# Products of constants on TensorE around the norms of a two-block transformer kernel

## The reference, cut to what matters

```python
# first block, per layer
h  = rms_norm(x, mix_norm_g[l]);  proj = h @ w_in[l]      # norm 0
...
x  = x + merged @ w_out[l]
h2 = rms_norm(x, mlp_norm_g[l])                            # norm 1
x  = x + square(relu(h2 @ w_up[l])) @ w_down[l]
# second block, per layer (a = 4 ** 0.25)
x = layer_norm(a * x + 0.5 * swiglu(x, ...), ...)          # norm 0
x = layer_norm(a * x + token_mixing(x, ...), ...)          # norm 1
x = layer_norm(a * x + cross_attention(x, mem, ...), ...)  # norm 2
x = layer_norm(a * x + 0.5 * swiglu(x, ...), ...)          # norm 3
```

## Time and profile before

| | |
|---|---|
| median of 3 runs | 2579.63 us (2578.45 to 2580.16) |
| profiled execution, first to last instruction | 2578.9 us |
| TensorE matmuls busy | 2391.2 us (93%), 16356 instructions |
| TensorE weight loads busy | 2194.2 us (85%), 16386 instructions |
| VectorE busy | 1418.0 us (55%) |
| ScalarE busy | 1146.1 us (44%) |
| GpSimd busy | 270.7 us (10%) |
| mean granted TensorE clock | 0.962 |

### The profile page before, as it was taken

One profiled execution on the slowest core, in us unless ns is written; L12 is line 12 of the kernel. 1 busy time (PEld: TensorE's weight loads), 2 busy tenths in 40 slices (PEclk: granted clock), 3 DMA queues, 4 the chain that ended last, 5 costly groups with the idle time before them and its releaser, 6 DMA issues.

```text
span 2578.9 us, 42911 instructions
## 1 busy us (share of the span) xinstructions
PE 2391.2 (93%) x16356; PEld 2194.2 (85%) x16386; DVE 1418.0 (55%) x1842; ACT 1146.1 (44%) x1792; POOL 270.7 (10%) x228
## 2 busy tenths in 40 slices
PE   6988998998999999899998889979999999987997
PEld 6978986887987998699997789879878999876996
DVE  4556555546654444555476564454465555765445
ACT  4744543663543443345343444434434434343443
POOL 0001200000110110100001221021110000221111
PEclk9999998999999999899998899989999999998998
DMA  6423554432553655334423335545544434252552
GB/s 201 146 83 117 186 193 146 164 115 82 178 185 140 216 183 191 136 137 174 163 100 131 131 128 183 199 154 187 198 143 166 159 108 169 81 175 95 181 197 98
DMA packets 56850, 394.46 MB, mean 153 GB/s; under 512 B 6678, under 2 KB 7040, under 8 KB 10944
## 3 DMA queue, kind: packets, MB, share of 16 engines
q1 hardware_dynamic: 52864, 377.98, 42.1%
q0 software_dynamic: 3776, 13.64, 1.7%
HBM read 391.24 MB, written 1.05 MB: 152 GB/s over the span
## 4 chain that ended last, share of the span: by engine, by line
PE 57%; DVE 4%; issue 4%; ACT 2%; DMA 0%; POOL 0%; DVEq 0%; SPq 0%; ACTq 0%; POOLq 0%
PE psum L372 51%; PE psum L691 2%; PE psum L721 2%; PE psum L1565 1%; PE psum L705 1%; DVE w_low L330 1%; ACT w_high L327 1%; PE psum L576 1%; DVE xT_low L629 0%; PE psum L398 0%; DVE gates L610 0%; DVE xs L1852 0%; DVE mx L747 0%; ACT attn_p L803 0%; DMA ring<-in_weights 0%
## 5 line engine op out<-in xcount | busy, mean ns | idle before, releaser
L330 DVE TENSOR_TENSOR w_low<-ring,w_high 128x1024 fp32r<-128x1024 f32 x704 | 882.3, 1279 | 647.8 <-ACT w_high L327 647.3
L372 PE MATMUL psum<-xT_high,w_high 128*128 128x256 f32 x3168 | 911.2, 288 | 35.4 <-DVE xT_low L629 20.9
L327 ACT ACTIVATE w_high<-ring 128x1024 fp32r<-128x1024 f32 x704 | 718.3, 1052 | 426.6 <-PE psum L372 390.3
L372 PE MATMUL psum<-xT_low,w_high 128*128 128x256 f32 x3168 | 905.0, 286 | 0.0
L372 PE MATMUL psum<-xT_high,w_low 128*128 128x256 f32 x3168 | 904.4, 285 | 0.0
L372 PEld LDWEIGHTS psum<-xT_high,w_high 128*128 128x128 f32 x3168 | 617.1, 195 | 39.0 <-DVE xT_low L629 19.6
L372 PEld LDWEIGHTS psum<-xT_low,w_high 128*128 128x128 f32 x3168 | 617.3, 195 | 0.2
L372 PEld LDWEIGHTS psum<-xT_high,w_low 128*128 128x128 f32 x3168 | 616.8, 195 | 0.0
L372 PE MATMUL psum<-w_high,hidden 128*128 128x512 f32 x1216 | 377.8, 390 | 9.7 <-DVE attn_pT L1841 5.2
L372 PEld LDWEIGHTS psum<-w_high,hidden 128*128 128x128 f32 x1216 | 228.2, 188 | 60.4 <-issue 11.8
L372 PE MATMUL psum<-w_low,hidden 128*128 128x512 f32 x608 | 236.6, 389 | 0.0
(11 more groups left out here) (212 smaller groups left out, 2284.9 us busy)
## 6 DMA issues: line engine op xcount, KB each, us to landing
ring<-in_weights SPq DMA_DIRECT2D x354, 1024.0 KB, 4.9
pages<-in_affine POOLq DMA_DIRECT2D x16, 512.0 KB, 5.9
ring<-in_weights SPq DMA_DIRECT2D x4, 880.0 KB, 4.4
pages<-in_mem POOLq DMA_DIRECT2D x2, 1024.0 KB, 5.2
x<-in_x_in SPq DMA_DIRECT2D x1, 1024.0 KB, 4.8
pages<-in_rows POOLq DMA_DIRECT2D x2, 512.0 KB, 7.3
y<-x SPq DMA_DIRECT2D x1, 1024.0 KB, 4.1
masks<-in_masks POOLq DMA_DIRECT2D x1, 640.0 KB, 8.3
```

What stands on the lines that cost most here:

```text
L327: eng.activation(high, raw, ACT.Copy).then_inc(*self.flag("w_rounded").one())
L330: eng.tensor_tensor(self.w_low[:, q % SPLITS, 0:w], raw, high.bitcast(F32), ALU.subtract).then_inc(*self.flag("w_split").one())
L372: m = pe.matmul(out, a, b, start=(first and i == 0), stop=(last and i == len(pairs) - 1))
```

## The change

A helper issues n matmuls of the constants. `norm_transposes` takes three counts: that many before the transposes of t = 0, before those of t = 1, and before the first products of the bank that comes next. Those around the transposes go to the columns of PSUM bank 7 from 256 + 128 t on, so they are 256 wide for t = 0 and 128 wide for t = 1; those after go to columns 0 to 255 of the bank that the next product group is about to write, behind the wait for that bank. All these columns are written again, with the accumulation started anew, before anything reads them. There is no new wait.

```diff
+        self.idle_after = 0
...
     def gemm_tokens(...):
         for t in range(NT):
             self.take_bank(pe, l, banks, (key, t))
+            self.next_bank_idle(pe, self.bank(banks, (key, t))[:, 0:SEQ])
...
     def gemm_features(...):
         out = self.bank(banks, group)
+        self.next_bank_idle(pe, out[:, 0:SEQ])
...
+    def idle_products(self, pe, out, n):
+        for _ in range(n):
+            pe.matmul(out, self.identb[:, :], self.masks[:, 0, 0:out.shape[1]], start=True, stop=True,
+                      skip_group_check=True)
-    def norm_transposes(self, pe, l, j, src):
+    def norm_transposes(self, pe, l, j, src, idle=(0, 0, 0)):
         for t in range(NT):
+            self.idle_products(pe, self.psum[:, 7, SEQ + t * P:2 * SEQ], idle[t])
             pe.wait_ge(*self.flag("xn_ready").at(l, NT * j + t + 1))
...
+        self.idle_after = idle[2]
+    def next_bank_idle(self, pe, out):
+        self.idle_products(pe, out, self.idle_after)
+        self.idle_after = 0
...
 # block 1
-            c.norm_transposes(pe, l, 0, c.xs)
+            c.norm_transposes(pe, l, 0, c.xs, (16, 30, 20))
-            c.norm_transposes(pe, l, 1, c.xs)
+            c.norm_transposes(pe, l, 1, c.xs, (4, 40, 16))
...
 # block 2
+            c.idle_after = 30
             ffn("f1", c.input_split(pe, l, None), 0)
-            c.norm_transposes(pe, l, 0, c.xs)
+            c.norm_transposes(pe, l, 0, c.xs, (4, 40, 28))
-            c.norm_transposes(pe, l, 2, c.xs)
+            c.norm_transposes(pe, l, 2, c.xs, (4, 40, 24))
-            c.norm_transposes(pe, l, 3, c.xs)
+            c.norm_transposes(pe, l, 3, c.xs, (4, 40, 0))
```

## The result

| | kernel before | changed kernel |
|---|---|---|
| median | 2578.45 us (7 runs, 2577.64 to 2580.16) | 2585.60 us (7 runs, 2583.88 to 2594.76) |
| profiled execution, first to last instruction | 2578.9 us | 2582.3 us |
| mean granted TensorE clock | 0.962 | 0.969 |

The ratio is 1.0032, with a 95% interval of 1.0022 to 1.0043: slower, 7.15 us in the medians, where 8.7 us of gain were forecast. The profiled execution of the changed kernel took 2583.88 us, the lowest of its seven. In all that follows, three executions that lay over 100 us above their neighbours are left out (3506.95 us of the changed kernel run again, 3276.78 and 2717.88 us of two others).

What follows compares the result with a forecast made beforehand. TensorE was taken to bound the kernel, its clock falling after waits at norms. Terms 2.8 + 1.1 + 1.7 + 0.4 + 2.7 + 0.8 - 0.8 gave 8.7 us gained, so 2570.9 us; range 2566 to 2576.

Steps and rivals of the forecast that it cites:

- Price of the constants: On TensorE at full clock, one product of constants takes 0.065 us for 128 columns and 0.12 us for 256; doubled when low.
- Rival 1: Products of 128 constant columns take 0.08 to 0.11 us, cutting the gain to 7.0 or 3.9; chance of 0.09 or more: 0.12.
- Start of the program: First products, of 512 columns, from 23.71 us: 14 run at full instead of low clock, gaining 2.8 us; lateness costs nothing.
- Norm 1 of block 1: Products after this norm run at full clock, less 0.4 us lateness: gains of 1.1 us in layer one, 1.7 in layer two.
- Norm 0 of layer two: In block 1: first product 1.6 us late, then full clock; net gain 0.4 us, between -0.5 and 2.0.
- Start of block 2: The first 28 products run at full clock, gaining 2.7 us; the 30 constants are covered by the wait for `w_low`.
- Norm 2: In block 2, twice: only the low stretch after the first products counts; 0.4 us gained each time, 0.8 in all.
- the fear that the text named: At norm 2 of block 2, TensorE idles 2 us twice, so the clock may fall again despite the 24 constants before.
- Norm 0 of block 2: Twice: faster products only lengthen the wait for `w_low` and the clock may fall; -0.8 us, between +0.5 and -1.6 for both.
- three signs of being wrong: Low stretches remaining at 238 and 646; t = 1 late by 1 us or more; `w_low` waits growing by what the norms gave.
- Rival 2: Weights or activations arrive no sooner and the clock falls elsewhere in block 2; half the sum goes, 2575.2 us; chance 0.17.
- Rivals 3 and 4: Constants fail to hold the clock up, near 28 us lost, 2607, chance 0.05; falls at norms have another cause, 2581, chance 0.04.

Runs made afterwards that it cites:

- after_again: The changed kernel run once more without any edit: nine executions, ratio 1.0029; the profiled execution took 2596.29 us.
- after_oc: The changed kernel plus nine 256-wide products of constants in the wait before `oc` in each layer of block 2: 2572.80 us, ratio 0.9976.
- the shifts: The kernel before with 4, 8 or 12 constants of 256 columns amid the `up` products of block 1: ratios 1.0029, 1.001 and 0.9989.

## Why the prediction was wrong, by its steps

**Price of the constants: right in kind, too high.** 0.056 us for 128 columns and 0.109 for 256 at the high clock, against 0.065 and 0.12. The first is below the lower bound of 0.06 that I had taken from half a product of 256 columns; the second was read off products of weights, which are slower (0.12). Rival 1 is out. The Trainium skill, "TensorE: Matmul & The Clock Gate", section "Back-to-back issue gap", states about 81 ns for sustained pairs; the forty pairs of this trace do not agree, with 56.

**Start of the program: right.** 2.8 us forecast; 2.75 by VectorE's fourth `w_low`, at 33.44 before and 30.69 after, and by TensorE's products from 34 us on.

**Norm 1 of block 1: clock right, size too high.** The prediction put the first four constants between the two sets of transposes; they lie ahead of both. From the first of them (226.94) to the transposes of t = 1 it is 3.56 us against 3.52, so the lateness was 0.04 and not 0.4. But products of weights at full rate ran into what feeds them: waits of 0.24 us for `xT_low` at 235.21 and 0.16 for `w_low` at 237.14. The lead grew by 0.5 us in layer one (forecast 1.1) and by 1.1 in layer two (1.7).

**Norm 0 of layer two: wrong low in this trace, nearer in others.** The forecast had t = 1 2.1 us late and the first product 1.6; from the first transposes to the first product it is 7.03 us against 6.87 before, 0.16 later. The lead grew by 2.1 us, about the upper bound that the text named (2.0), and not by 0.4, since the 30 constants took 2.3 us and not the 3.4 of the forecast, and the 20 behind them ran beside the evacuation. It depends on when the clock comes back, for which the prediction took 2.8 us of constants without a row that shows it: in the trace of after_again the same 30 take 3.20 us (423.73 to 426.93) and the first product comes 1.4 us late. Of the nine traces with block 1's constants, six have it 1.1 to 1.5 us late and gain 0.6 to 1.1 us here, and three have it in place.

**Start of block 2: right** in its place, 2.65 against 2.7 (a lead of 8.06 us becomes 10.7).

**Norm 2: nothing, where 0.8 was forecast.** The idle times are 1.79 and 1.81 us with the 24 constants done in between, and the low stretch is there again at 1494.20: the fear that the text named came true in full.

**Norm 0 of block 2: right sign, too small.** The wait for `w_low` in layer one grew from 2.18 us to 3.48, as the text had it, and the lead stayed 10.7 us. In layer two the wait grew from 1.36 to 2.62, and with the falls behind it 4.1 us went, where the bound for both layers was -1.6. This was no accident of one trace: all seven with these constants lose 4.1 to 4.3 us there.

These terms make 2.75 + 0.5 + 1.1 + 2.1 + 2.65 = 9.1 us. The other 1.6 us of the lead at 848 us came from low stretches in the attentions of block 1 that went away or moved: one at 87.87 us of before brought 1.57 us. The prediction counted none of these.

Summed up, the trace has 10.7 us won, 4.1 lost behind norm 0 and 9.5 at the compressors, and 0.5 in small steps: 3.4 us slower in the span, where 8.7 faster were forecast.

**The step that failed** is the sentence behind the sum: "Behind each of these places TensorE is dense and is what VectorE and ScalarE wait for, so a gain stays." A gain of time stayed for 1050 us. What did not stay was the clock in stretches that the change does not touch. The sum took each of them as fixed, as the one profile showed it. They are not fixed: of 89 executions of the kernel before, 23 lie 10 us higher (none of 7, then 13 of 31, 4 of 18, 4 of 23, 2 of 10). The three executions that I had were all of the lower kind, in which both layers pass the wait before `oc` at full clock; the trace showed these compressors at 1.00, and nothing in it showed how near they are to falling. The changed kernel has at least one layer hit in each of its 16 executions, by their times; two profiles confirm it, with one and two.

Where nine constants hold this place (after_oc) the change comes to 2572.80 us, inside the range of 2566 to 2576. The second step that failed is the term of norm 0 in block 2, -0.8 for both layers, which measured -4.1 in layer two alone.

None of the three signs of being wrong that the text named has come: the low stretches at 238 and 646 are gone, t = 1 is 0.04 us late, and the waits for `w_low` fell from 21.3 to 14.7 us. They all watched the places of the change, and the loss lay elsewhere.

**Rival 2** ("Clock kept, gain lost behind it ... the clock falls in the attentions and norms of block 2 at other places than before") was right in its second half, with the wrong price; the waits for `w_low` did not take the gain. I let it take half of the sum and so kept it above no change. A fall costs what follows it: 9.5 us here, more than the sum. Rivals 3 and 4 are out: the constants do hold the clock up, and the text's loss of 28 us does not appear.

**What stays open.** Why the phase of the changed kernel hits a compressor every time: the shifts show that 0.9 us can do it, not why. Why norm 0 of block 2 costs 4.1 to 4.3 us in layer two of every trace and 1.1 to 1.8 us between medians: the stretch that gives 2.9 us back in two traces is seen, not what makes it go. Whether the 16 products of 64 columns (1.89 us) that stand ahead of the wait before `oc` have a part in the falls: no run changed them. Whether the one-row bias products (L400, 1.74 us at 1896.81) lead to the falls at 1900.28, 1917.34 and 1944.42, which begin while TensorE is busy: no run left them out.

## What to carry to other kernels

When a stretch of narrow products follows a short wait, fill that wait first: nine products of constants in 1 us were worth 9.5 us in a hit layer, more than the 6.2 us that the norms together bring when that place is held. Count such fillers as the length of the wait over their measured spacing (0.109 us for 256 columns), and only where what follows is bound by TensorE. Before summing gains of the clock, run the kernel before some 20 times and shift it by a microsecond: if its times fall into groups, one profile shows one of them, and a small gain can change which.

## What was unexpected of the hardware

- Full TensorE activity did not mean full clock. The 64x15 products of a compressor ran at busy 1.00 and a granted clock of 0.50 for 13.15 us, and the whole low stretch, with transposes ahead and 5.3 us of wide products behind, lasted 20.5 us; the low stretches of the earlier trace rows, of wide products alone, last 3.23 to 6.04 us. The same 128 products ran at 1.00 for 6.89 us where they were entered at it.
- The same 1.02 us wait for the same tile is followed by a fall of the clock in 9 of 20 cases. The Trainium skill, "TensorE: Matmul & The Clock Gate", section "What's actually happening", says that the ramp depends on the run and costs under 1% of a typical kernel. The groups here, 10 us or 0.4% apart, agree with both, though they come from falls in the middle of the kernel; they are larger than the change.
- Pairs of a weight load and a bfloat16 product of 128 columns sustain 0.056 us, half of the 0.109 us for 256 columns.
- Mean granted clock and time can part: in the two profiled executions 0.962 to 0.969 with 3.4 us more. Twice the missing share of the span is the time at half clock: 2 x 0.038 x 2578.9 = 196 us before and 2 x 0.031 x 2582.3 = 160 after. 36 us less of it did not shorten the run. The 20.5 us that are new at the compressor lie over dense work and cost 9.5; so some 56 us of low clock went elsewhere. Over dense work they would be worth half as much, 28 us; 10.7 were won by 848 us, and the rest lay over waits or was lost again.
